# Retention as items of the attention's stream, and an output projection that takes y column by column

## The reference

```python
def step(S, inp):                       # retention, one chunk
    qc, kc, vc = inp
    scores = jnp.einsum('bihd,bjhd->bhij', qc, kc) * decay_mask[None]
    inner = jnp.einsum('bhij,bjhe->bihe', scores, vc)
    cross = jnp.einsum('bihd,bhde->bihe', qc, S) * q_decay
    S_new = S * chunk_decay + jnp.einsum('bjhd,bjhe->bhde', kc * k_decay, vc)
    return S_new, inner + cross

def mixer_merge(x, o_a, g_a, o_b, o_c, lam_init, subln_g, w_out, g, b):
    ya = rms_norm(o_a).reshape(B, T, H_A * DV_A) * jax.nn.silu(g_a.astype(jnp.float32))
    yc = rms_norm(o_c, subln_g) * (1.0 - lam_init)
    y = jnp.concatenate([ya, o_b.reshape(B, T, H_B * DH_B), yc.reshape(B, T, H_C * DV_C)], -1).astype(x.dtype)
    return layer_norm(DEEPNORM_ALPHA * x + y @ w_out, g, b)
```

## Time and profile before

| what | value |
|---|---|
| median of 3 runs | 1866.9 us (1862.1 to 1869.56) |
| the profiled execution's own time | 1871.24 us |
| its span, first to last instruction | 1869.6 us |
| granted TensorE clock, mean | 0.964 |
| TensorE, VectorE, ScalarE busy | 1743.7, 927.0, 667.6 us |
| DMA | 319.40 MB, mean 171 GB/s |

### The profile page before, as it was taken

The page is one execution under the profiler, slowest core; times in us unless marked ns, Lnnn a source line. Parts: engine busy times, 40 slices in busy tenths (PEclk is TensorE's granted clock), DMA queues, the critical chain, the costliest instruction groups (busy, mean ns, idle before and its releaser), DMA issues.

```text
span 1869.6 us, 29845 instructions
## 1 busy us (share of the span) xinstructions
PE 1743.7 (93%) x12302; PEld 1595.1 (85%) x12302; DVE 927.0 (50%) x1497; ACT 667.6 (36%) x929; POOL 114.8 (6%) x220
## 2 busy tenths in 40 slices
PE   7999999977899799999999999997779988999997
PEld 6999999745789589999999999985468876999997
DVE  5545354534564464553464544554545533645534
ACT  3432233333253243333243332423423432433323
POOL 0000100000000000001100001000000000000010
PEclk9999999988799999999999999998979998999998
DMA  7433464588136633433434434538742564334342
GB/s 244 149 143 131 145 221 151 175 311 318 71 137 202 256 150 135 157 134 133 165 130 139 154 124 150 223 130 299 301 196 102 187 225 192 110 142 157 127 142 75
DMA packets 62898, 319.40 MB, mean 171 GB/s; under 512 B 8922, under 2 KB 11354, under 8 KB 37706
## 3 DMA queue, kind: packets, MB, share of 16 engines
q0 software_dynamic: 31104, 205.53, 31.0%
q1 hardware_dynamic: 31690, 112.36, 16.1%
HBM read 307.08 MB, written 10.79 MB: 170 GB/s over the span
## 4 chain that ended last, share of the span: by engine, by line
PE 84%; DVE 6%; DMA 5%; ACT 3%; issue 1%; SPq 1%; DVEq 0%; ACTq 0%
PE ps L578 21%; PE ps L580 21%; PE ps L579 21%; PE ps L545 4%; PE ps L694 2%; PE ps L696 2%; PE ps L695 2%; DMA ring<-in_wkv 2%; PE ps L881 1%; DMA ring<-in_ckv 1%; DVE bn L1413 1%; PE ps L908 1%; PE ps L692 1%; PE ps L691 1%; DMA cache<-in_ckv 1%
## 5 line engine op out<-in xcount | busy, mean ns | idle before, releaser
L578 PE MATMUL ps<-x_high,w_high 128*128 128x320 f32 x1408 | 437.3, 311 | 1.6 <-DVE w_low L1358 1.6
L579 PE MATMUL ps<-x_low,w_high 128*128 128x320 f32 x1408 | 436.2, 310 | 0.0
L580 PE MATMUL ps<-x_high,w_low 128*128 128x320 f32 x1408 | 436.1, 310 | 0.0
L1069 ACT ACTIVATE w_high<-ring 128x2048 fp32r<-128x2048 f32 (+1 forms) x152 | 256.8, 1691 | 469.9 <-PE ps L580 468.8
L1358 DVE TENSOR_TENSOR w_low<-ring,w_high 128x2048 fp32r<-128x2048 f32 (+1 forms) x152 | 305.7, 2011 | 140.2 <-ACT w_high L1069 140.0
L578 PEld LDWEIGHTS ps<-x_high,w_high 128*128 128x128 f32 x1408 | 265.4, 188 | 3.6 <-DVE w_low L1358 2.6
L579 PEld LDWEIGHTS ps<-x_low,w_high 128*128 128x128 f32 x1408 | 265.3, 188 | 0.0
L580 PEld LDWEIGHTS ps<-x_high,w_low 128*128 128x128 f32 x1408 | 265.3, 188 | 0.0
L514 POOL DMA_DIRECT2D ring<-in_w x216 | 114.6, 531 | 1718.1 <-PE ps L580 1233.7
L578 PE MATMUL ps<-h_high,w_high 128*128 128x320 f32 x704 | 219.9, 312 | 0.0
L580 PE MATMUL ps<-h_high,w_low 128*128 128x320 f32 x704 | 217.5, 309 | 0.0
(11 more groups left out here) (287 smaller groups left out, 2440.9 us busy)
## 6 DMA issues: line engine op xcount, KB each, us to landing
ring<-in_w POOLq DMA_DIRECT2D x152, 1024.0 KB, 5.1
ring<-in_w POOLq DMA_DIRECT2D x64, 704.0 KB, 4.2
cache<-in_dkv SPq DMA_DIRECT2D x64, 256.0 KB, 6.1
ring<-in_dkv SPq DMA_DIRECT2D x64, 256.0 KB, 4.2
cache<-in_ckv SPq DMA_DIRECT2D x8, 2048.0 KB, 10.5
ring<-in_ckv SPq DMA_DIRECT2D x8, 2048.0 KB, 7.8
cache<-in_wkv SPq DMA_DIRECT2D x8, 1536.0 KB, 9.0
ring<-in_wkv SPq DMA_DIRECT2D x8, 1536.0 KB, 7.9
```

The source lines that it names most:

```text
L578: mm(out, wh, xh, start=first, stop=False)
L579: mm(out, wh, xl, start=False, stop=False)
L580: return mm(out, wl, xh, start=False, stop=last)
L1069: fn(w_high[:, pos % 2, 0:n], ring[:, pos % RING, 0:n], ACT.Copy).then_inc(hi_w.sem, 1)
```

## The change

Retention becomes items of the list, with kinds of their own that have no softmax (`PLAIN`). Their first products are "scores" in bank 3 (and 4), which VectorE takes over in `maxima`; ret_head and ret_dec have values in bank 7 too, which ScalarE squares and copies (`rows`). The merge of y (`merge`) is what remains after the list. y's columns are transposed into six banks of their own, and the first chunk of the output projection waits before each k for that column alone. A new tile, `spare`, holds what retention needs beside the attention's tiles, and later the first out slot; the size of the DMA scratch is given to the build.

```diff
-MIXER = [("diff_dec", 0), ("win_pro", 0), ("win_pro", 1), ("diff_dec", 1), ("win_pro", 2), ("diff_dec", 2),
-         ("win_pro", 3), ("diff_dec", 3)] + [(k, g) for g in range(4) for k in ("diff_pro", "win_dec")]
+MIXER = [("diff_dec", 0), ("win_pro", 0), ("win_pro", 1), ("ret_turn", 0), ("diff_dec", 1), ("win_pro", 2), ("ret_head", 0),
+         ("ret_rows", 0), ("diff_dec", 2), ("win_pro", 3), ("ret_head", 1), ("ret_new", 0), ("diff_dec", 3), ("diff_pro", 0),
+         ("ret_head", 2), ("diff_own", 0), ("win_dec", 0), ("ret_head", 3), ("ret_dec", 0), ("diff_pro", 1), ("ret_state", 0),
+         ("win_dec", 1), ("diff_pro", 2), ("ret_state", 1), ("win_dec", 2), ("diff_pro", 3), ("ret_state", 2),
+         ("ret_state", 3), ("win_dec", 3)]
...
+Y_BANKS = (1, 2, 3, 4, 6, 7)
...
+        spare = sb("spare", [P, 3584])
...
+        out_slot = spare[:, 0:2048]
+        qx = spare[:, 0:1024].rearrange("p (h g t) -> p h g t", h=HX, g=4)
+        kx = spare[0:NS, 2304:2816].rearrange("p (h b d) -> p h b d", h=HX, b=2)
...
@@ sync
+                sp.wait_ge(m_done.sem, m_done.upto(l, scored("ret_new", 0)))
+                sp.dma_start(layer_of(o["s_pro"], l), view(s_pro, [[1, 512]])).then_inc(out_st.sem, 16)
+                sp.wait_ge(m_done.sem, m_done.upto(l, scored("ret_state", 3)))
+                sp.dma_start(layer_of(o["s_dec"], l), view(s_dec, [[1, 2048]])).then_inc(out_st.sem, 16)
                 cross_pair(0)
-                wait_apart(sp, "sp", st_act.sem, st_act.upto(l, 1))
-                sp.dma_start(layer_of(o["s_pro"], l), view(s_pro, [[1, 512]])).then_inc(out_st.sem, 16)
-                sp.wait_ge(st_dve.sem, st_dve.upto(l, 4))
-                sp.dma_start(layer_of(o["s_dec"], l), view(s_dec, [[1, 2048]])).then_inc(out_st.sem, 16)
@@ gpsimd
                     if pos == POS_MIX + HEAD:
-                        pool.wait_ge(o_psum.sem, o_psum.upto(l, after("win_dec", 3)))
+                        pool.wait_ge(o_psum.sem, o_psum.upto(l, given("ret_dec", 0)))
+                        load(name, pos % RING, pos, index[name], out_slot)
+                        pos, index[name] = pos + 1, index[name] + 1
+                        continue
+                    elif pos == POS_MIX + HEAD + 1:
+                        pool.wait_ge(o_psum.sem, o_psum.upto(l, given("win_dec", 3)))
@@ tensor
+                            if q0 + m == H_OUT:
+                                pe.wait_ge(y_low.sem, y_low.upto(l, (1, 2, 3, 4, 5, 5, 6, 7)[k]))
...
+                    elif kind == "ret_head":
+                        r = 64 * (n % 2)
+                        q, k = qTp[r:r + 64, n // 2, :], kTp[r:r + 64, n // 2, :]
+                        mm(ps[:, 3, 0:256], k[:, 0:128], q, start=True, stop=True)
+                        last = mm(ps[:, 3, 256:384], k[:, 128:256], q[:, 128:256], start=True, stop=True)
...
+                    elif kind == "ret_state":
+                        pe.wait_ge(kx_built.sem, kx_built.upto(l, n + 1))
+                        for h in range(HX):
+                            last = mm(ps[:, 3, P * h:P * h + P], view(kx[:, h, 0, 0:1], [[1, P]]),
+                                      tmat(0, NS, 2, 512 + P * h, P), start=True, stop=True)
...
+                    if kind in ("ret_head", "ret_dec"):
+                        pe.wait_ge(m_done.sem, m_done.upto(l, i + 1))
+                        pe.wait_ge(o_done.sem, o_done.upto(l, OUTS[i] - 1))
...
-                        transposes(i, first)
+                        if SOFT[i]:
+                            transposes(i, first)
...
-                        values(i, first)
+                        if i == 0 or OUTS[i] > OUTS[i - 1]:
+                            values(i, first)
@@ scalar
+                def rows(i):
+                    kind, n = ITEMS[i]
+                    act.wait_ge(o_psum.sem, o_psum.upto(l, OUTS[i]))
+                    if kind == "ret_head":
+                        for g in range(2):
+                            fn(scrap[g], ps[:, 7, P * g:P * g + P], ACT.Square, accum_out=small[:, 12 + 4 * g + n:13 + 4 * g + n])
+                        last = fn(ytok[:, 0:2, P * n:P * n + P], ps[:, 7, 0:2 * P].rearrange("p (g e) -> p g e", g=2), ACT.Copy)
+                    else:
+                        for h in range(HX):
+                            fn(lp[0:NS, P * h:P * h + P], ps[0:NS, 7, P * h:P * h + P], ACT.Square, accum_out=small[0:NS, 20 + h:21 + h])
+                        last = fn(ytok[0:NS, 2, 0:512], ps[0:NS, 7, :], ACT.Copy)
+                    last.then_inc(o_done.sem, 1)
...
                 act.wait_ge(rss_done.sem, rss_done.upto(l, 1))
                 fn(small[:, 24:48], small[:, 0:24], ACT.Sqrt).then_inc(rsd_done.sem, 1)
                 high_half(H_OUT)
                 act.wait_ge(out_st.sem, out_st.upto(l, 32))
@@ vector
+                        if ITEMS[i] == ("diff_pro", 3):
+                            head_squares()
...
+                def merge():
+                    dve.wait_ge(rsd_done.sem, rsd_done.upto(l, 1))
+                    link(V.reciprocal(small[:, 24:48], small[:, 24:48]))
+                    for h in range(HX):
+                        for g in range(3):
+                            w = min(P, T - P * g)
+                            y = ytok[0:w, g, P * h:P * h + P]
+                            last = V.scalar_tensor_tensor(y, y, small[0:w, 36 + 4 * g + h:37 + 4 * g + h],
                                                           tmat(0, w, g, 1024 + P * h, P), ALU.mult, ALU.mult)
+                        last.then_inc(ya_done.sem, 1)
...
+                    dve.wait_ge(oc_psum.sem, oc_psum.upto(l, 1))
+                    V.tensor_copy(ob[:, 4:6, SEQ:T], ps[:, 5, 0:2 * NS].rearrange("p (c t) -> p c t", c=2)).then_inc(ob_done.sem, 1)
                     low_half(H_OUT)
...
-    nc = _bacc.Bacc("TRN2", target_bir_lowering=False, num_devices=1)
+    nc = _bacc.Bacc("TRN2", target_bir_lowering=False, num_devices=1, dynamic_dma_scratch_size=2048)
```

More of the change, by code:

```diff
@@ L67 @@
 assert SLOTS % RING == 0
-MIXER = [("diff_dec", 0), ("win_pro", 0), ("win_pro", 1), ("diff_dec", 1), ("win_pro", 2), ("diff_dec", 2),
-         ("win_pro", 3), ("diff_dec", 3)] + [(k, g) for g in range(4) for k in ("diff_pro", "win_dec")]
+MIXER = [("diff_dec", 0), ("win_pro", 0), ("win_pro", 1), ("ret_turn", 0), ("diff_dec", 1), ("win_pro", 2), ("ret_head", 0),
[3 more added lines that the diff above has]
+         ("ret_state", 3), ("win_dec", 3)]
 CROSS = [(k, g) for g in range(4) for k in ("cross_dec", "cross_pro")]
 ITEMS = MIXER + CROSS
-NI = len(ITEMS)
-BATCHES = [{"diff_dec": 3, "win_dec": 2}.get(k, 1) for k, _ in ITEMS]
+NI, NM = len(ITEMS), len(MIXER)
+PLAIN = ("ret_turn", "ret_rows", "ret_head", "ret_dec", "ret_new", "ret_state", "diff_own")
+BATCHES = [0 if k in PLAIN else {"diff_dec": 3, "win_dec": 2}.get(k, 1) for k, _ in ITEMS]
 BEFORE = [sum(BATCHES[:i]) for i in range(NI)]
 NB = sum(BATCHES)
-DECODE = [k[-3:] == "dec" for k, _ in ITEMS]
-PROMPTS = [DECODE[:i + 1].count(False) for i in range(NI)]
+DECODE = [k in ("diff_dec", "win_dec", "cross_dec") for k, _ in ITEMS]
+SOFT = [k not in PLAIN for k, _ in ITEMS]
+EXPS = [sum(SOFT[:i + 1]) for i in range(NI)]
+OUTS = [sum(k not in PLAIN or k in ("ret_head", "ret_dec") for k, _ in ITEMS[:i + 1]) for i in range(NI)]
+PROMPTS = [sum(f and not d for f, d in zip(SOFT[:i + 1], DECODE)) for i in range(NI)]
 SCORES_AT = [0 if d else 3 for d in DECODE]
-DVE_STEPS = 99
+NE, NO = EXPS[-1], OUTS[-1]
+DVE_STEPS = 98
 CHUNK_DECAY = [float(np.float32(np.exp(DT * np.log1p(-2.0 ** (-5.0 - h))))) for h in range(HX)]
+Y_BANKS = (1, 2, 3, 4, 6, 7)
 class Signal:
@@ L356, in entry, with given, scored, slot @@
             return place[:, base + at:base + at + w]
-        def after(kind, g):
+        def given(kind, g):
+            return OUTS[ITEMS.index((kind, g))]
+        def scored(kind, g):
             return ITEMS.index((kind, g)) + 1
+        def slot(pos):
+            return out_slot if pos == POS_MIX + H_OUT // 2 else ring[:, pos % RING, :]
         def half_done(eng, l, q):
@@ L458, in cross_pair @@
                         if g == 0 and b2 == 0:
-                            sp.wait_ge(o_psum.sem, o_psum.upto(l, after("win_dec", 2)))
+                            sp.wait_ge(o_psum.sem, o_psum.upto(l, given("win_dec", 2)))
                         elif g == 1:
@@ L1032, in _ @@
                 attention(0, len(MIXER), rows_out)
-                retention()
+                merge()
                 project(1, H_OUT)
@@ L1205, in attention @@
                     for i in range(first, end):
-                        copies(i)
-                        if i + 1 < end:
+                        if SOFT[i]:
+                            copies(i)
+                        if i + 1 < end and SOFT[i + 1]:
                             exponentials(i + 1)
+                        if ITEMS[i][0] in ("ret_head", "ret_dec"):
+                            rows(i)
                         if i + 2 == NI:
```

(17 more changed lines are left out.)

340 lines of the change are left out of this document (144 added, 196 removed).

## The result

The changed kernel takes 1900.6 us (median; 1893.3 to 1903.5), beside 1867.5 us for the kernel before on the same chip: ratio 1.0176, 95% interval 1.0139 to 1.0213. It is **slower by 1.8%**, 32 us above the forecast of 1869 us and outside its range (1858 to 1876, and 1848 to 1891 for 8 in 10). The interval leaves no doubt that it is slower; whether by 2% it leaves open.

A forecast was written before the change was run, and what follows sets the result against it. TensorE, busy 93%, was taken as the bound. Full-clock savings of 16 us against 18 of lower clock gave +2 on the profiled 1871.24, which lies 4.3 over the median: 1869 us, range 1858 to 1876 (8 in 10: 1848 to 1891).

The forecast's parts named there:

- Tail 46.5 to 8.7 us: From the mixer attention's last matmul to the output projection's first: 46.5 us shrink to 8.7, saving 37.8 a layer.
- No price for the moved loads: Out-slot loads and state outputs, issued at new points, cost nothing; up to 5 us a layer if the cover fails.
- Seven uncovered exponentials, near 15 us a layer: In the mixer attention, decode transposes wait 2.7 to 3.2 us for ScalarE's exponential, near 15 us a layer.
- Stream 107.3 us at full clock: First decode item's end to the mixer attention's last matmul: seven intervals sum to 107.3 us, against 78.2 and 76.8.
- the 2.5 us in which ScalarE was to free bank 7: In the last window decode interval, 2.5 us until ScalarE has squared and copied its result, part of 19.7 us.
- I take 0.90, near the stream's own: Granted clock assumed for the lengthened mixer attention: 0.90, against 0.91 before, since scores and values stand between waits.
- 44 us a layer: Extra time if all work on TensorE's path in the new mixer attention ran at 1.2 GHz: 44 us a layer.
- The term of 9 us a layer, 18 in all: Clock cost in the lengthened mixer attention: 20% of 44 us, so 9 us a layer, 18 in all.
- Rival 2: Uncovered decode waits in the mixer attention drop TensorE to 1.2 GHz for values and next scores: 1891 us, chance 0.24.
- The size of a fall: Clock drop at a decode item: 1.3 us for its values, chance one in two; up to 4.8 us an interval.
- Rival 3: Weights or the state's output land late before the output projection, 5 to 8 us a layer: 1882 us, chance 0.04.
- rival 4: DMA scratch of 2048 holds back loads that POOL issues, at most some 10 us: 1880 us, chance 0.02.

The follow-up runs named there:

- half filling: The changed kernel plus 4 or 3 dummy products ahead of each of seven waits for exponentials: 1881.8 us, ratio 1.0063 to the kernel before.
- the filling: The changed kernel plus 8 or 6 dummy products ahead of each of seven waits for exponentials: 1867.0 us, ratio 1.0018 to the kernel before.
- short filling: The changed kernel plus 3 or 2 dummy products between each mixer item's transposes and values, long waits left empty: 1869.1 us, ratio 0.999 to the kernel before.
- the reordering: The changed kernel with scores of the next softmax item and its first retention item ahead of the previous item's transposes: 1841.9 us, ratio 0.9884 to the kernel before.
- the transposes: The changed kernel plus 16 or 12 dummy identity transposes ahead of each of seven waits for exponentials: 1866.9 us, ratio 0.9997 to the kernel before.

## Why the prediction was wrong

Point by point, by its own steps:

- *Tail 46.5 to 8.7 us*: right, 8.1 in both layers, and by the terms given: output 0.48, reciprocal 0.29, products 3.23, decode heads' products 0.41, low_half 1.21. (The terms listed add up to 7.8, not 8.2; with 0.5 for semaphores that is 8.3.)
- *No price for the moved loads*: right; TensorE's waits name no DMA in the stream, and the output projection begins as expected, without one.
- *Seven uncovered exponentials, near 15 us a layer*: right, 14.4 in seven waits.
- *Stream 107.3 us at full clock*: some 7 us a layer too long. Taking half of the busy time at the low level off the measured stream leaves 132.7 - 33.1 = 99.6 and 126.2 - 26.1 = 100.1 us. One term is seen to be absent: the 2.5 us in which ScalarE was to free bank 7 is no wait of TensorE's in either layer. The record doesn't say how the rest is spread.
- *"I take 0.90, near the stream's own"*, and 44 us a layer as what would double: **this is the step that failed**. The clock was 0.72 and 0.76. The reason given for 0.90, that scores and values still stand between the waits, didn't hold the clock: 66 of the 104 us that TensorE is busy in layer 0's stream ran at the low level. And at the full clock the stream has some 71 us of busy time that doubles, not 44. The term of 9 us a layer, 18 in all, was 33 and 26, or 59: 41 too little, of which the stream that was too long hid 15. With the prediction's own 44 the measured shares, 56% and 48%, give 107.3 + 24.6 = 131.9 and 128.4, near the measured 132.7 and 126.2; that is **luck**, two errors that cancel, and no proof of either term. With the measured ones the forecast's own sum is -16 - 15 for the shorter stream - 1 for the tail + 59 = +27 on 1871, or 1898, the profiled execution's time.
- Rival 2, "the clock decides the other way", is what happened. Its turning point, a low share of 28%, was passed by far (56% and 48%), and even its price at 45%, 20 us a layer, was short of the truth. The upper bound that the prediction had written down, the clock of 0.71 of the stretch behind the list, was the nearer row; 0.91 was that of a stream whose exponentials were covered.
- *The size of a fall* is where the term went wrong. Falls behind uncovered waits came as rival 2 had them: in both layers all seven decode items ran their values wholly or in part at the low level. The prediction priced a fall at the values, 1.3 us, once in two, and at most at an interval's 4.8 (its terms add up to 4.9). Measured, a low stretch held 2.8 to 13.7 us of busy time (1.4 to 6.8 us lost, by the estimate above) and reached into the retention products and the next item's scores. It also counted no fall for the prompt items' longer waits for VectorE, which it did put in the stream's length; in layer 0 three of the nine begin there.
- *Rival 3* (late loads) didn't happen; *rival 4* (the scratch) explains 2.5 us by the medians and 9 at most by the interval, not 33.

Where did the expected gain go? It came: 37.8 us of tail a layer were saved as forecast, and idle time fell by 4.5 us in all. It was given back in the clock, 32 us of slower matmuls beside the kernel before, which itself ran a third of these two parts at the low level. The half filling, the filling, the short filling and the reordering all move time and clock together, with the same matmuls of the kernel in them, so that is shown. What rule takes the clock down and back up is not: waits of 2.3 us were mostly followed by a fall but not always, some falls had only waits of 1.0 or 0.4 us with 0.6 us ahead of them, and no run here isolates it.

## What to carry to other kernels

Compare busy time and count of the same instructions before and after, not only idle time: here idle fell while the same 1090 matmuls took 18.5 us longer. When work is interleaved into a pipelined stream, look first at which latency the stream's order was covering; an item without transposes and values of its own, put ahead of an item with a long softmax, takes its cover away, and the clock can cost twice what the waits do (here an estimated 33 and 26 us a layer beside 14.4 us of waits). Then ask the table of stretches for the low ones: how many there are, how long each lasts, and what idle time stands before and in it. Where a wait can't be covered, cheap products into a free bank are a quick test of whether the clock is the cost, and here even an improvement. Check a sum by its terms: a total that fits can be two errors.

## What was unexpected in the hardware

- 48 dummy products a layer made the changed kernel some 30 us faster, and dummies of 0.5 to 0.8 us at the short waits alone did too, although 17.6 us of long waits stayed.
- A single wait of 2.3 us, with work for 5 us ahead of it and dense work behind it (the second diff_dec item with the dummies behind the waits), was followed by a fall of the clock in both layers. Nine low stretches held 75.1 us in the changed kernel and 34.1 with dummies behind the waits: their length was the loss, not their number.
- The same idle total goes with very different clocks: 34 to 36 us a layer at 0.84 in the kernel before, 32 to 33 at 0.72 and 0.75 in the changed one, 35.6 at 0.87 with dummies behind the waits.
- Transposes held the clock as well as products.
- The clock also differs between executions of nearly the same code: layer 1's stretch, 134.3 us at 0.84 in the kernel before, is in the profile of the one with the smaller scratch

```profile
1275.67:1419.96 144.29, 111.09 (x1090) 75.75 (x1091) 63.84 (x231) 46.68 (x136) 2.11 (x4) 0.75 0.67 252
```

10 us longer at 0.75, with idle of 33.2 us as before (34.1). A single profile of this kernel can thus be some 10 us off by the clock, while the medians of the two kernels lie 2.5 us apart. The profiles of half the filling, the short filling and the transposes were each the slowest execution of their kernel, so the clocks read from them are low rather than high.
